# An encoder step on one core: gate work moved on GpSimd, the keys' second turning a step later, and the sample's first output product moved into the last head

## The reference

```python
def sb_attend(q, k, v, q_pos, k_pos):
    z = jnp.einsum("bqhd,bkhd->bhqk", q, k) * (HEAD_DIM ** -0.5)
    mask = k_pos[None, :] < q_pos[:, None]
    log_1m = jnp.where(mask, jax.nn.log_sigmoid(-z), 0.0)
    suffix = lax.cumsum(log_1m, axis=3, reverse=True) - log_1m
    a = jnp.where(mask, jnp.exp(jax.nn.log_sigmoid(z) + suffix), 0.0)
    return jnp.einsum("bhqk,bkhd->bqhd", a, v)

def merge(oa, za, ob, zb, gn_a, gn_b, w_out):
    ya = rmsnorm(oa, gn_a) * jax.nn.silu(za)
    yb = rmsnorm(ob, gn_b) * jax.nn.silu(zb)
    return jnp.einsum("bte,ed->btd", jnp.concatenate([ya, yb], axis=-1), w_out)

xp = xp + merge(...)            # prompt
xs = xs + merge(...)            # sample
y_prompt, y_sample = rmsnorm(xp, final_norm_g), rmsnorm(xs, final_norm_g)
```

## Time and profile before

| | |
|---|---|
| time before, median of 3 runs | 1086.44 us (1084.65 to 1087.22) |
| the profiled execution's own time | 1085.68 us |
| its span, first to last instruction | 1083.9 us |
| PE busy | 1020.3 us, 94% |
| DVE busy | 668.3 us, 62% |
| ACT busy | 465.2 us, 43% |
| POOL busy | 262.5 us, 24% |
| mean granted clock of TensorE | 0.992 |

### The profile page before, as it was taken

One profiled execution on the slowest core, in us unless ns is written; L12 is line 12 of the kernel. 1 busy time (PEld: TensorE's weight loads), 2 busy tenths in 40 slices (PEclk: granted clock), 3 DMA queues, 4 the chain that ended last, 5 costly groups with the idle time before them and its releaser, 6 DMA issues.

```text
span 1083.9 us, 27357 instructions
## 1 busy us (share of the span) xinstructions
PE 1020.3 (94%) x11316; PEld 859.8 (79%) x11316; DVE 668.3 (62%) x979; ACT 465.2 (43%) x911; POOL 262.5 (24%) x198
## 2 busy tenths in 40 slices
PE   6899999999999999999999998999879999888997
PEld 5898778986679898889888897777767777776786
DVE  5557445664566646556655515767677777776487
ACT  5522311222112132322332215766777777676353
POOL 2300000000000011011211015000355566666496
PEclk9999999999999999999999999999999999999999
DMA  6366797798888888778988778555624243321343
GB/s 225 108 238 226 248 331 263 292 362 304 322 298 340 308 312 293 309 269 307 349 332 300 252 224 276 133 145 116 146 49 99 61 105 79 78 59 50 136 156 137
DMA packets 121329, 234.02 MB, mean 216 GB/s; under 512 B 60537, under 2 KB 91257, under 8 KB 103809
## 3 DMA queue, kind: packets, MB, share of 16 engines
q1 hardware_dynamic: 95872, 209.33, 57.1%
q10 hardware_dynamic: 25344, 23.08, 6.2%
HBM read 204.52 MB, written 27.86 MB: 214 GB/s over the span
## 4 chain that ended last, share of the span: by engine, by line
PE 71%; POOL 9%; DVE 7%; issue 7%; ACT 3%; DMA 1%; ACTq 0%; DVEq 0%; SPq 0%; POOLq 0%
PE bank L887 28%; PE bank L874 8%; PE bank L951 7%; PE bank L997 6%; PE bank L1666 4%; PE bank L1246 4%; PE bank L1199 3%; PE bank L1222 3%; POOL pr L1546 3%; PE bank L980 3%; DVE om L1478 2%; DVE pr L1468 2%; POOL za L1642 1%; PE bank L1261 1%; DMA k_buf<-in_cache_sb_k 1%
## 5 line engine op out<-in xcount | busy, mean ns | idle before, releaser
L887 PE MATMUL bank<-w_hi,hT_hi 128*128 128x256 f32 (+1 forms) x896 | 261.1, 291 | 3.7 <-DVE hT_lo L620 3.3
L887 PE MATMUL bank<-w_lo,hT_hi 128*128 128x256 f32 (+1 forms) x896 | 253.5, 283 | 0.5 <-issue 0.5
L887 PE MATMUL bank<-w_hi,hT_lo 128*128 128x256 f32 (+1 forms) x896 | 253.1, 282 | 0.0
L887 PEld LDWEIGHTS bank<-w_hi,hT_hi 128*128 128x128 f32 x896 | 171.0, 191 | 11.1 <-issue 5.4
L887 PEld LDWEIGHTS bank<-w_lo,hT_hi 128*128 128x128 f32 x896 | 171.2, 191 | 0.8 <-issue 0.7
L887 PEld LDWEIGHTS bank<-w_hi,hT_lo 128*128 128x128 f32 x896 | 171.0, 191 | 0.0
L534 ACT ACTIVATE u_out<-bank 128x256 f32<-128x256 f32 x112 | 43.0, 384 | 271.8 <-PE bank L887 271.5
L730 DVE STREAM_TRANSPOSE k_buf<-k_buf 128x2048 f32<-128x2048 f32 x64 | 145.3, 2292 | 5.7 <-DMA k_buf<-in_cache_sb_k 5.4
L1478 DVE TENSOR_TENSOR_SCAN om<-om 128x1024 f32<-128x1024 f32 (+3 forms) x64 | 115.8, 1818 | 16.8 <-ACT om L1378 16.2
L1222 PE MATMUL bank<-ident,pr 128*128 128x128 f32 x576 | 88.4, 282 | 22.9 <-POOL pr L1546 18.5
L1546 POOL TENSOR_TENSOR pr<-pr,om 128x1023 f32<-128x1023 f32 (+3 forms) x64 | 89.7, 1410 | 80.2 <-DVE om L1478 80.2
(11 more groups left out here) (203 smaller groups left out, 1941.0 us busy)
## 6 DMA issues: line engine op xcount, KB each, us to landing
k_buf<-in_cache_fox_k SPq DMA_DIRECT2D x32, 1024.0 KB, 9.1
v_ring<-in_cache_fox_v SPq DMA_DIRECT2D x32, 1024.0 KB, 6.6
k_buf<-in_cache_sb_k SPq DMA_DIRECT2D x32, 1024.0 KB, 9.4
v_ring<-in_cache_sb_v SPq DMA_DIRECT2D x32, 1024.0 KB, 7.0
w_raw<-in_w_in SPq DMA_DIRECT2D x14, 1024.0 KB, 9.3
out<-u_out ACTq DMA_DIRECT2D x72, 128.0 KB, 5.2
q_scratch<-u_out ACTq DMA_DIRECT2D x64, 128.0 KB, 5.6
k_nat<-out SPq DMA_DIRECT2D x32, 256.0 KB, 3.9
```

The costliest lines, as they stand in the source:

```text
L887: mm = pe.matmul(bank[:, U + i % 2, w_cols(c)], a[:, k, hcols(s)], b[c % 2][:, k, w_cols(c)], start=(k == 0 and n == 0), stop=(k == KD - 1 ...
```

## The change

1. On POOL, in each sb head, `a_gain` stands right behind `a_silu`, both after the product of unit 1; before, the product of unit 2 stood between them. In the first sb head both stand after unit 3. `a_root` moves from after unit 3 to after unit 7.
2. In the sb heads the second half of the keys' turning moves from step 2 to step 3, on PE, and with it its high part on ACT (to step 4) and its low part on DVE (to step 3). The fox heads keep theirs.
3. The gates of rounds 0 and 1: `b_gate` moves on ACT to step 5 of heads 14 and 15, `b_silu` and `b_gain` on POOL to the end of these heads. So round 0 is ready when head 15 begins; its turning, high and low part stand at steps 1 and 2 of head 15, and its two half products before the turnings of units 3 and 4 of head 15. Before, the round's turning was at step 5, and its product behind all of head 15. Its results now go to PSUM banks 1 and 3.
4. At the end of head 15, ACT makes the gates of rounds 2 and 3 at once, PE turns round 2 and then makes round 1's product, and the last half of head 15 is turned after it. DVE takes `b_gain` of rounds 2 and 3 and `b_out` of round 0 ahead of the last `store_o`.
5. On SP, the load of the last `za` goes behind the first four gate loads of the merge.

```diff
-        PREP_AT = {1: 0, 2: 1}
+        PREP_AT = ({1: 0, 2: 1}, {1: 0, 3: 1})
...
             for p in range(NPAIR - 1, 2 * NPAIR - 1):
                 next_pair(p, 1)
-            load_a(sp, TP - 1)
...
+                    if following is None and u in (3, 4):
+                        b_product(pe, 0, (u - 3,))
...
-                    if u in PREP_AT and following:
-                        turn_k_of(pe, *following, PREP_AT[u])
+                    if u in PREP_AT[g] and following:
+                        turn_k_of(pe, *following, PREP_AT[g][u])
...
-                    if u in (5, 7) and following is None:
-                        b_turn(pe, u // 7)
+                    if following is None and u == 1:
+                        b_turn(pe, 0)
+                    if following is None and u == 7:
+                        b_turn(pe, 1)
...
-            b_product(pe, 0)
+            b_turn(pe, 2)
+            b_product(pe, 1, (0, 1))
             turn(NHEAD - 1, 1, last=True)
...
-                    if u == 6 and following is None:
+                    if u == 5 and isinstance(h, int) and h >= NHEAD - 2:
+                        b_gate(act, h - (NHEAD - 2))
+                    if u == 2 and following is None:
                         b_high(act, 0)
...
-                    if u in (0, 2) and following is None:
-                        b_gate(act, u // 2)
...
             run_pairs(act, start, pair)
+            b_gate(act, 2)
+            b_gate(act, 3)
+            a_move(act, NHEAD - 1, 1)
+            b_high(act, 1)
             move_o(NHEAD - 1, 1)
-            b_high(act, 1)
-            a_move(act, NHEAD - 1, 1)
+            b_high(act, 2)
...
             run_pairs(dve, start, pair)
+            b_gain(dve, 2)
             b_low(dve, 1)
+            b_gain(dve, 3)
             dve_merge_first(dve)
             store_o(2 * NPAIR - 1, 1, 1, 1)
...
-                    if u == 3:
-                        a_root(pool, h)
                     if u == (3 if h == NHEAD // 2 else 1):
                         a_silu(pool, h)
-                    if u == (4 if h == NHEAD // 2 else 2):
                         a_gain(pool, h)
-                    if h == NHEAD - 1 and u in (2, 6):
-                        b_silu(pool, u // 6)
-                    if h == NHEAD - 1 and u in (3, 7):
-                        b_gain(pool, u // 7)
+                    if u == NU - 1:
+                        a_root(pool, h)
+                    if h >= NHEAD - 2 and u == NU - 1:
+                        b_silu(pool, h - (NHEAD - 2))
+                        b_gain(pool, h - (NHEAD - 2))
...
             for r in range(TP):
                 if r == 4:
+                    load_a(sp, TP - 1)
                     sp.wait_ge(pv_done, NU * (NHEAD - 1) + 4)
                 load_z(r)
...
         def dve_merge_first(dve):
             b_mean(dve, 0)
-            b_gain(dve, 2)
             b_mean(dve, 1)
+            b_low(dve, 2)
+            b_out(dve, 0, 0)
+            b_out(dve, 0, 1)
...
         def pool_merge(pool):
             b_silu(pool, 2)
+            b_silu(pool, 3)
             b_root(pool, 0)
             b_root(pool, 1)
-            b_silu(pool, 3)
             b_root(pool, 2)
```

More of the change, by code:

```diff
@@ L252, in build @@
         zb = place(AT_K + 12288, "zb", [P, TP, W], F32)
-        yT_hi = place(AT_H, "yT_hi", [P, 2, NPAIR, P], F32R)
-        yT_lo = place(AT_H + 4096, "yT_lo", [P, 2, NPAIR, P], F32R)
+        yT_hi = [place(AT_H + 4096 * i, f"yT_hi{i}", [P, NPAIR, P], F32R) for i in range(2)]
+        yT_lo = [place(AT_H + 4096 * i + 2048, f"yT_lo{i}", [P, NPAIR, P], F32R) for i in range(2)]
         fg_b = place(AT_H + 8192, "fg_b", [P, D], F32)
@@ L1410, in pair @@
                         move_odd(h, 0)
-                    if u - 1 in PREP_AT and following:
-                        split_k(act, *following, PREP_AT[u - 1])
+                    if u - 1 in PREP_AT[g] and following:
+                        split_k(act, *following, PREP_AT[g][u - 1])
                     if u == MOVE_AT:
@@ L1515, in pair @@
                         store_o(p, hh, 0, g)
+                    if u == 2 and following is None:
+                        b_low(dve, 0)
                     if ahead:
                         (scans if g_ahead else maxima)(*ahead)
-                    if u in PREP_AT and following:
-                        prep(*following, PREP_AT[u])
+                    if u in PREP_AT[g] and following:
+                        prep(*following, PREP_AT[g][u])
                     if g and u == 1:
                         a_mean(dve, h)
-                    if u == 6 and following is None:
-                        b_low(dve, 0)
             def start():
@@ L1784, in b_high, with b_product @@
             if r < 2:
-                act.wait_ge(sc_ready, NU * NHEAD)
+                act.wait_ge(sc_ready, NU * (NHEAD - 1 + r))
             else:
                 act.wait_ge(yp_ready, 2 * (r - 1))
-            act.activation(yT_hi[:, r % 2], in_four(bank[:, turn_bank(r), :]), ACT.Copy).then_inc(yhb_done, 1)
+            act.activation(yT_hi[r % 2][:], in_four(bank[:, turn_bank(r), :]), ACT.Copy).then_inc(yhb_done, 1)
         def b_low(dve, r):
             dve.wait_ge(yhb_done, r + 1)
-            dve.tensor_tensor(yT_lo[:, r % 2], in_four(bank[:, turn_bank(r), :]), yT_hi[:, r % 2].bitcast(F32), ALU.subtract
+            dve.tensor_tensor(yT_lo[r % 2][:], in_four(bank[:, turn_bank(r), :]), yT_hi[r % 2][:].bitcast(F32), ALU.subtract
                               ).then_inc(ylb_done, 1)
-        def b_product(pe, r):
+        def b_product(pe, r, parts):
             pe.wait_ge(ylb_done, r + 1)
-            if r < 2:
+            if r == 0:
+                pe.wait_ge(s_moved, NU * NHEAD - 4)
+                pe.wait_ge(wolo_done, 4)
+            if r == 1:
                 pe.wait_ge(s_moved, NU * NHEAD)
-                pe.wait_ge(wolo_done, 4)
-            for n, (at, wide) in enumerate(columns_of(r)):
+            for n in parts:
+                at, wide = columns_of(r)[n]
                 if r >= 2:
-                    pe.wait_ge(xo_done, 2 * (r - 2) + at // W + 1)
-                three_products(pe, product_of(r, n), yT_hi[:, r % 2], yT_lo[:, r % 2],
+                    pe.wait_ge(xo_done, 2 * (r - 2) + at // W + 1 + (r == 2 and n == 1))
+                three_products(pe, product_of(r, n), yT_hi[r % 2], yT_lo[r % 2],
                                NPAIR * int(r > 0), slice(at, at + wide)).then_inc(yp_ready, 1)
@@ L1999, in pe_merge @@
         def pe_merge(pe):
-            for r in range(1, NR):
+            for r in range(2, NR):
                 if r + 1 < NR:
                     b_turn(pe, r + 1)
-                b_product(pe, r)
+                b_product(pe, r, range(len(columns_of(r))))
         block_ = keep.enter_context(nc.Block())
```

17 lines of the change are left out of this document (7 added, 10 removed).

## The result

The changed kernel takes 1093.03 us (median of 7 runs, 1091.12 to 1098.8), the kernel before beside it 1085.55 (7 runs): ratio 1.0069, 95% interval 1.0050 to 1.0087. The change is slower by 0.7%; the forecast was 1092.0. The profiled execution has a span of 1089.6 us, 5.7 more than before.

What follows compares the result with a forecast made beforehand. PE was busy 94% of the span, so only its idle time, mostly waits for POOL's products, and slow clock could be won. Heads 0 + 0, clock 6.0, head 14 to 15 1.3, merge -2.0, last head 1.0: +6.3, 1092.0 us; range 1083 to 1098.

Steps and rivals of the forecast that it cites:

- Part 1 and 2, the heads: sb heads: waits of 1.39 and 0.91 us become one of 2.4 before x6; 0.0 a head, bounds -0.4 to +0.2.
- my signs of being wrong: Changed profile: scans and gates overlapping, the long wait leaving the clock alone, or heads getting shorter would show the prediction wrong.
- the faster rival: sb heads: DVE and POOL don't exclude each other as read, 1.2 us less a head, 1074.6; chance 0.19 with an in-between case.
- The sentence behind it: POOL and DVE on SBUF: after one POOL instruction a waiting scan goes first, even if POOL's next is ready.
- The clock: Middle heads and end of the first: 4 falls to 1.2 GHz behind long waits, 1.5 us each, +6.0 (0 to 12).
- Head 14 to 15: Between heads 14 and 15: round 0's gate work on POOL holds up head 15's first scan, +1.3 us.
- Head 15 and the merge: Last head and merge: PE's waits shrink but POOL's chain limits the gain, -2.0; a low clock stretch adds 1.0.
- x6 waits as in the other heads: Head 15: product 2 comes 1.33 us later, b_turn fills 0.35, so x6 waits 2.6 us.
- The cap by POOL's chain: Merge: rounds 4 to 9 on POOL need 31.1 us of bare work, so only 2.0 of PE's 4.0 us are won.
- one of my signs: Merge in the changed profile: PE would be seen waiting for the inputs of rounds 6 to 9.
- Its other foot: Head 15: 5.58 us of PE waits do go; in-between case with all 4.0 us won in the merge, 1080.6.
- Sum: Whole kernel: all terms add to +6.3 us on the profiled execution's 1085.68, giving 1092.0, +0.5% on the median.

Runs made afterwards that it cites:

- the one-column run: The changed kernel with `a_gain` multiplying one column of 512 instead of all; 1072.84 us, ratio 0.9883 to the kernel before.
- the filled wait: The changed kernel with unit 5's score matmuls issued four times before x6 in each sb head; 1085.58 us, ratio 0.9996 to the kernel before.
- the run with the early gate: The kernel before with parts 3 to 5, and round 0's `b_gate` ahead of the fox rows' high part on ACT in head 14; 1083.28 us, ratio 0.9970.
- parts 1 and 2 alone: The kernel before with only parts 1 and 2 of the change; 1088.68 us, ratio 1.0028 to the kernel before.
- parts 3 to 5 alone: The changed kernel with parts 1 and 2 taken back; 1084.25 us, ratio 0.9985 to the kernel before.

## Why the prediction was right, and where it was not

- **Part 1 and 2, the heads.** I had one wait of 2.4 for 1.39 + 0.91 and 0.0 a head: the wait was 2.0 to 2.28, and a head without a fall is 0.2 shorter, inside my bounds of -0.4 and +0.2. (Shorter heads stood among my signs of being wrong; 0.2 is not what the faster rival needs, 1.2.) The order that I laid on head 12 (scan 2, gain, scan 3, product 2) is what the trace shows. The sentence behind it, that a waiting scan goes ahead of POOL's next, holds for instructions of 512 columns; the one-column run shows its limit. The Trainium skill, "SBUF — State Buffer", section "Who interferes with whom", has the exclusion, and the trace agrees (2.55 us for a gain of 1.27). In the first sb head I had 0 (-0.3 to +1.5): it costs about 1.3, which the profile hides behind a low stretch that happened to be missing.
- **The clock.** Four falls at 1.5 = +6.0: three at 1.6 = +4.84. That these falls and not the later product are the loss in the heads is shown by the filled wait.
- **Head 14 to 15.** +1.3: +1.1 in the profile, by the mechanism given; in the run with the early gate all of it is gone.
- **Head 15 and the merge.** -2.0 + 1.0 = -1.0: +0.33. The step that failed is "x6 waits as in the other heads", for which I had 2.6 us. It waited 4.12. The 1.1 us by which POOL and DVE were late against PE put the scan of unit 2 ahead of `a_silu`, and one more scan stood before product 2. I had worked out both delays and not that one changes the order in the other. The runs bear this out: with parts 1 and 2 alone `a_silu` takes 1.28 and x6 waits 2.56; with parts 3 to 5 alone `a_silu` takes 2.73 but no gain stands before product 2, and x6 waits 2.01; the two together give 4.12.
- **The cap by POOL's chain.** It was too tight. Counted from head 15's unit 1, round 4's `b_silu` comes 0.7 earlier with parts 3 to 5 alone, where I had it 1.4 later, and from there to round 9's it takes 30.1 us, where I had 31.1. The tail is 4.35 less, more than my 4.0 for PE itself, of which I had worked out only 5.58 - 3.95 = 1.63 as waits. PE waiting for the inputs of rounds 6 to 9, one of my signs, does not show: it is busy for 46.8 of the 47 us from 1031 to 1078 in the changed kernel.
- **Faster rival.** It needed scans and gates to overlap; they do not. Its other foot, 5.58 us of waits in head 15 to be won, was real and shows in parts 3 to 5 alone.
- **Sum.** +6.3 forecast, +5.7 in the profile, +7.5 between the medians. The sum is better than its terms, and that is luck: the clock was 1.15 too dear, the heads 1.1 and head 14 to 15 0.2; the tail was 1.3 too cheap, and 0.55 of the 5.7 lie outside my terms, in unchanged code and the first head.

## What to carry to other kernels

Where two engines take turns on SBUF, an instruction costs its work and the other side's that gets in behind it: put such work behind the products for which the bottleneck waits, not merely next to other work of its kind. Look at the lengths of waits, not only their sum: two short ones and a long one of the same total are not the same when the clock falls behind the long one. Compare profiles head by head, and note how many low stretches each execution has and where. And work out two edits together where both reach the same stretch; here they took 2.7 and 4.35 us off the tail alone, and together they added 0.33.

## What the runs showed of the hardware

- The same wait was followed by 1.2 GHz in one head and not in another: one of 2.25 us in heads 11 and 13 was, one of 2.23 in head 12 was not, in both profiles of the changed kernel. What decides between them stays open.
- A fall behind x6 in heads 9 to 14 lasts about 3.4 us and costs 1.6 us, where PE has little slack. Where PE waits anyway it costs less: 1.4 us for 6.8 us at 0.50 in the first sb head, and 0.6 us for 6.8 in place of 3.4 in head 15.
- 1.5 us of repeated matmuls a head made the kernel 6.6 us faster.
- A POOL instruction of 128x1 that had waited for a scan let POOL's next instruction follow after 0.09 us, ahead of DVE's next scan; behind one of 128x512 the next scan went first.
